# Attention probabilities turned in halves of 64 query rows, one half to each PSUM bank

## The reference

```python
s = jnp.einsum('bgrqd,bgkd->bgrqk', q, kc).astype(jnp.float32) * scale
p = jax.nn.softmax(s, axis=-1) if sink is None else softmax_with_sink(s, sink)
o = jnp.einsum('bgrqk,bgkd->bgrqd', p.astype(vc.dtype), vc)
```

## Time and profile before

| | before |
|---|---|
| median of three runs | 2024.0 us |
| profiled execution | 2020.81 us, its span 2018.9 us |
| TensorE matmul busy | 1805.2 us, 89% |
| TensorE weight load busy | 1390.1 us, 69% |
| VectorE busy | 1046.3 us, 52% |
| ScalarE busy | 606.0 us, 30% |
| GpSimd busy | 325.4 us, 16% |
| mean granted TensorE clock | 0.943 |

### The profile page before, as it was taken

The page is one execution under the profiler, slowest core; times in us unless marked ns, Lnnn a source line. Parts: engine busy times, 40 slices in busy tenths (PEclk is TensorE's granted clock), DMA queues, the critical chain, the costliest instruction groups (busy, mean ns, idle before and its releaser), DMA issues.

```text
span 2018.9 us, 26641 instructions
## 1 busy us (share of the span) xinstructions
PE 1805.2 (89%) x9754; PEld 1390.1 (69%) x9754; DVE 1046.3 (52%) x1994; ACT 606.0 (30%) x910; POOL 325.4 (16%) x416
## 2 busy tenths in 40 slices
PE   7869879899949999999899968997989689999994
PEld 1737546566838888888678856884667578887883
DVE  1535645574385676666544356266753534344442
ACT  1201035464332112211223333113543423233342
POOL 0231312232150000000000033014421400000002
PEclk9889989999969999999999988997999889999997
DMA  7665643112242443344221163334512333332233
GB/s 263 161 155 188 241 94 98 40 25 88 81 146 84 125 119 102 112 125 125 84 73 63 63 231 124 103 112 119 134 34 74 104 92 95 104 86 70 85 103 115
DMA packets 258124, 223.99 MB, mean 111 GB/s; under 512 B 67470, under 2 KB 218271, under 8 KB 258038
## 3 DMA queue, kind: packets, MB, share of 16 engines
q1 hardware_dynamic: 249156, 202.50, 33.2%
q0 software_dynamic: 7008, 18.79, 3.3%
q10 hardware_dynamic: 1876, 1.58, 0.3%
HBM read 193.58 MB, written 29.25 MB: 110 GB/s over the span
## 4 chain that ended last, share of the span: by engine, by line
PE 76%; DVE 11%; POOL 4%; issue 3%; DMA 3%; ACT 2%; SPq 0%; ACTq 0%; DVEq 0%; POOLq 0%
PE ps L995 31%; PE ps L676 9%; PE ps L677 9%; PE ps L678 9%; PE ps L848 4%; PE ps L890 4%; PE ps L927 3%; PE ps L690 2%; POOL arena L1832 2%; DVE arena L1604 2%; DVE arena L1568 1%; DVE arena L1396 1%; PE ps L719 1%; PE ps L700 1%; PE ps L882 1%
## 5 line engine op out<-in xcount | busy, mean ns | idle before, releaser
L1331 DVE TENSOR_TENSOR w_lo<-w_raw,w_hi 128x2048 fp32r<-128x2048 f32 (+3 forms) x114 | 209.6, 1839 | 353.0 <-ACT w_hi L1082 352.9
L676 PE MATMUL ps<-w_hi,act_hi 128*128 128x512 f32 (+2 forms) x952 | 371.9, 391 | 18.7 <-DVE act_lo L1331 17.8
L677 PE MATMUL ps<-w_lo,act_hi 128*128 128x512 f32 (+2 forms) x952 | 368.8, 387 | 0.0
L678 PE MATMUL ps<-w_hi,act_lo 128*128 128x512 f32 (+2 forms) x952 | 368.3, 387 | 0.0
L1082 ACT ACTIVATE w_hi<-w_raw 128x2048 fp32r<-128x2048 f32 (+3 forms) x114 | 176.6, 1550 | 552.0 <-PE ps L678 434.4
L995 PE MATMUL ps<-act_hi,w_hi 128*128 128x512 f32 (+1 forms) x1056 | 321.0, 358 | 2.8 <-DVE act_lo L1331 2.8
L995 PE MATMUL ps<-act_lo,w_hi 128*128 128x512 f32 (+1 forms) x1056 | 319.7, 357 | 0.0
L995 PE MATMUL ps<-act_hi,w_lo 128*128 128x512 f32 (+1 forms) x1056 | 319.2, 356 | 0.0
L676 PEld LDWEIGHTS ps<-w_hi,act_hi 128*128 128x128 f32 x952 | 182.7, 192 | 58.1 <-issue 15.8
L678 PEld LDWEIGHTS ps<-w_hi,act_lo 128*128 128x128 f32 x952 | 182.2, 191 | 34.7
L677 PEld LDWEIGHTS ps<-w_lo,act_hi 128*128 128x128 f32 x952 | 182.4, 192 | 34.0
(11 more groups left out here) (108 smaller groups left out, 1835.4 us busy)
## 6 DMA issues: line engine op xcount, KB each, us to landing
arena<-in_ada_w SPq DMA_DIRECT2D x44, 1024.0 KB, 8.7
w_raw<-in_ffn_up SPq DMA_DIRECT2D x88, 512.0 KB, 5.3
w_raw<-in_ffn_down SPq DMA_DIRECT2D x88, 256.0 KB, 2.7
w_raw<-in_odd_w_in SPq DMA_DIRECT2D x20, 512.0 KB, 4.6
arena<-mods SPq DMA_DIRECT2D x16, 512.0 KB, 6.7
proj_odd<-arena POOLq DMA_DIRECT2D x26, 256.0 KB, 2.5
x_after_mix<-arena SPq DMA_DIRECT2D x10, 512.0 KB, 2.9
arena<-x_after_mix SPq DMA_DIRECT2D x10, 512.0 KB, 4.2
```

Of the source, the lines that this page charges most:

```text
L676: mm(out_, s_hi, m_hi, start=start, stop=False)
L677: mm(out_, s_hi, m_lo, start=False, stop=False)
L678: return mm(out_, s_lo, m_hi, start=False, stop=stop)
L1331: V.tensor_sub(out_, full, hi.bitcast(fp32)).then_inc(sem_, 1)
```

## The change

The transposes of probabilities no longer split the key tiles over the two banks. Each tile is transposed in two parts: query rows 0 to 63 through array rows 0 to 63 into bank 6, and query rows 64 to 127 through array rows 64 to 127 into bank 7. Each part is a 64 by 128 stationary operand against a 64 by 64 identity. A bank then holds n pieces of 64 columns. Both banks are waited for ahead of the first part, and the two parts of the last tile signal the two banks. ScalarE and VectorE each copy n times 64 columns, into the 64-column halves of the tiles in SBUF. The preparation rounds are as they were.

```diff
@@ probs_t (TensorE)
                     v = (sunk if a.name == "swa" else biased)[k % 2][x][:, ROWS - n * P:ROWS]
-                    srcs = [v[:, c * P:(c + 1) * P] for c in range(n)]
-                    turns(a.unit_round[k, x], srcs[:(n + 1) // 2], srcs[(n + 1) // 2:])
+                    r = R0 + a.unit_round[k, x]
+                    at_least(pe, left_free, r)
+                    at_least(pe, right_free, r)
+                    for c in range(n):
+                        for g in range(2):
+                            half = slice(64 * g, 64 * g + 64)
+                            last = nc.tensor.transpose(bank(6 + g)[:, c * 64:(c + 1) * 64],
+                                                       v[half, c * P:(c + 1) * P], ident[half, half])
+                            if c == n - 1:
+                                last.then_inc((left_done, right_done)[g], 1)
@@ attention (ScalarE)
+                def left_rows(r, dst, n):
+                    act.wait_ge(left_done, R0 + r + 1)
+                    A(dst, bank(6, n * 64).rearrange("p (t r) -> p t r", r=64), ACT.Copy).then_inc(left_free, 1)
 ...
                 def probs(k, x):
-                    n = (len(keys_of(a.units[a.steps[k][1]])) + 1) // 2
+                    n = len(keys_of(a.units[a.steps[k][1]]))
                     at_least(act, pv_done, PV0 + V0 + k - 1)
-                    left(a.unit_round[k, x], pt[k % 2][x][:, 0:n, :].rearrange("p t r -> p (t r)"), n)
+                    left_rows(a.unit_round[k, x], pt[k % 2][x][:, 0:n, 0:64], n)
@@ attention (VectorE)
+                def right_rows(r, dst, n):
+                    dve.wait_ge(right_done, R0 + r + 1)
+                    V.tensor_copy(dst, bank(7, n * 64).rearrange("p (t r) -> p t r", r=64)).then_inc(right_free, 1)
 ...
-                    right(a.unit_round[k, x], pt[k % 2][x][:, (n + 1) // 2:n, :].rearrange("p t r -> p (t r)"), n // 2)
+                    right_rows(a.unit_round[k, x], pt[k % 2][x][:, 0:n, 64:128], n)
```

## The result

The change makes the kernel slower. Its median is 2041.03 us (2038.64 to 2042.62, four runs) against 2023.96 (2019.84 to 2025.72) for the kernel before beside it: ratio 1.0086, 95% interval 1.0067 to 1.0106. The forecast was 2035, in a range of its own of 2028 to 2042. The profiled execution took 2039.48, 18.7 more than the one of before; forecast were 10.9 more.

The account below looks back on a forecast made before the run. TensorE was the only engine near full, with waits between engines setting most steps. NA 5.1, SWA 8, MLA 0.4, GQA -0.6 and phase ends -2 made +10.9 on 2020.8: 2031.7, or 2035 on the median's scale, range 2028 to 2042.

Parts of the forecast that it names:

- The price of a record: Transposes of probabilities: a 64-row record takes 0.033 us, so six key tiles take 0.40 instead of 0.66.
- Rival A: Transposes in all four phases: halves don't pay in full, 0.053 us a record, 13 us more, 2048; chance 0.2.
- rival B: Transposes in all four phases: no overlap at all, 0.107 us a record, 75 us in all, 2099; chance 0.08.
- The wait: Head 1's turn moves behind VectorE's copy, delaying ScalarE's copy and exp: NA +5.1, SWA +8 us.
- the NA loop: NA's regular step: the loop through ScalarE takes 5.28 us against 4.96, +0.32, in ten of 16 steps.
- SWA's regular pair: SWA's six steps of a pair: together 2.0 us longer, four pairs +8.
- MLA's pair: MLA: small preparation steps lose 0.38 each, large steps gain 0.56 over two; three pairs at +0.2 us, phase +0.4.
- The drain: TensorE between array shapes: 0.09 to 0.15 us a change; in GQA four added changes a step, 0.45 together.
- GQA's sign: GQA steps: shorter turns outweigh the added shape changes, -0.07 us a step, -0.6 in all.
- The ends of the phases: Last two turns of each of four phases, with no minima in their way: each saves 0.26 us, -2 in all.
- Rival C: Attention phases: ScalarE's delay is absorbed and shorter turns pay on the path, faster at 2008; chance 0.08.
- D: Whole kernel: nothing measurable, 0.027 us a record and SWA's delay half hidden, +7, 2026; chance 0.14.

Follow-up runs that it names:

- the kernel with halves in turn: The changed kernel, but each head's row-0-to-63 records come first, waiting for bank 6 alone, then the others for bank 7: 2024.44 us, ratio 1.0014.
- the filler's run: The changed kernel plus a useless TensorE product ahead of head 1's turn in 40 of 48 MLA and SWA steps: 2051.17 us, ratio 1.0138.
- the whole-transposes run: The changed kernel in MLA, SWA and NA, with whole 128-row transposes in GQA: 2045.17 us, ratio 1.0101.
- e8: As e7, but head 0 alternates the row halves while head 1 keeps them in turn: 2025.97 us, ratio 1.0001.
- e7: The changed kernel with row halves one after the other, each waiting for its own bank, in MLA, SWA, NA; whole transposes in GQA: 2024.88 us, ratio 0.9997.

## Why the prediction was right, and where its sizes were off

**The price of a record** came out as taken. Twelve take 0.56 to 0.59 and one 0.223, (0.56 - 0.223)/11 = 0.031 to 0.033; 0.033 was taken. That it fits so closely is in part luck: the eight 32-row products of the earlier trace rows do not come at an even pace, they start as four at 343.84 and four at 344.05, and their 0.033 is the mean of one such gap. Rival A (0.053) and rival B (0.107) fall here. The rule that spoke for A, in the Trainium skill (TensorE: Matmul & The Clock Gate, LDWEIGHTS: a load's time is its columns over 1.2 GHz, by estimate 0.107 for 128 columns), is not what these loads show: six in a row in one half, in the kernel with halves in turn, are (0.45 - 0.139)/5 = 0.062 apart by their loads.

```profile
1457.28 0.45 PEld L910 LDWEIGHTS ps<-ident,arena 64*128 64x128 f32 x6 [0.17 <-issue]
```

**The wait** did what was said, and three runs show it from three sides: without the joint wait, with it alone, and with the exp out of its reach. By terms the NA loop was 2.28 + 0.55 + 0.06 + 0.80 + 0.39 + 1.04 + 0.16 = 5.28 forecast, and is 2.29 + 0.55 + 0.15 + 0.65 + 0.39 + 1.05 + 0.08 = 5.16. Turn to copy was put 0.15 too long: the 0.43 for a first record held the long form's own 0.27, where the short one's is 0.22, and it was read to VectorE's copy, which starts 0.05 behind ScalarE's. The start behind the copy was put 0.09 too short, the reciprocal 0.08 too long. NA steps with a preparation of Q grew by 0.28 and with one of K by 0.35 (forecast 0.25 and 0.37).

SWA's regular pair grew by 1.7 (forecast 2.0), and its steps one by one agree too: 0.46, 0.15, 0.27, 0.50, 0.48 and -0.17, against 0.37, 0.18, 0.37, 0.57, 0.51 and 0. (The step that the prediction calls two-key and bound by the outputs' copies turns four keys.) MLA's pair grew by 0.1 (forecast 0.2), which is the difference of larger parts: the two small steps with a preparation grew by 0.42 and 0.38 (forecast 0.38 each), the other four shrank by 0.70 together (forecast 0.56).

**The drain** was undersized, and that turned GQA's sign. A step's two turns last 0.52 each, of which 12 x 0.031 = 0.37 are records and 0.15 is not, and PV and the scores are 0.20 longer each: the four changes are 0.70, not 0.45, and the step is +0.12, not -0.07. The starts of single records tell where it lies. Ahead of a turn, PV's last product starts at 1543.13 and the first transpose at 1543.33, 0.21 apart instead of 0.11. Behind a turn, the last transpose starts at 1540.30, PV's first product at 1540.46 and its second at 1540.67; those two are 0.21 apart instead of 0.11. So entering costs 0.10, and leaving 0.15 and then 0.10 more behind the first product. The prediction took 0.09 to 0.15 a change from rows read only up to the first product behind it. The Trainium skill (TensorEngine Tiling (Array Packing), Key Properties) says that a change of mode drains the engine, and this trace agrees; here a turn pays 0.35 for its two changes.

**The ends of the phases** were to give 2 us and gave none that can be seen; at the end of GQA TensorE waits for VectorE's copy twice, 0.84 us each, where before it waited 0.41 for ScalarE's and 0.81 for VectorE's.

**The clock** is what the sum left out, and the prediction had named its fall as a cause outside it. Mean granted clock and the engines' busy time in the four phases, before and after (columns: stretch, its length, busy us and instructions of each engine, clock, DMA share, GB/s):

```profile
266.00:394.00 128.00, 119.55 (x1117) 78.21 (x1117) 70.63 (x206) 65.44 (x158) 36.62 (x48) 0.99 0.27 62
396.00:490.00 94.00, 85.71 (x724) 56.26 (x724) 63.17 (x219) 57.56 (x154) 31.49 (x48) 0.96 0.10 23
1386.00:1483.00 97.00, 87.14 (x738) 57.33 (x738) 61.89 (x202) 51.14 (x107) 43.24 (x39) 0.94 0.34 86
1486.00:1549.00 63.00, 56.76 (x366) 45.16 (x366) 28.81 (x70) 25.34 (x53) 14.49 (x16) 1.00 0.00 1
```

```profile
267.30:395.90 128.60, 106.58 (x1340) 72.26 (x1340) 69.48 (x205) 65.58 (x158) 36.62 (x48) 0.97 0.27 62
398.70:500.80 102.10, 74.36 (x900) 56.12 (x900) 62.64 (x217) 57.52 (x154) 31.49 (x48) 0.92 0.10 21
1395.80:1498.70 102.90, 73.89 (x930) 55.45 (x930) 60.72 (x202) 51.09 (x107) 43.09 (x39) 0.90 0.33 82
1502.10:1567.00 64.90, 57.23 (x462) 43.02 (x462) 27.97 (x69) 25.55 (x53) 14.48 (x16) 0.98 0.00 1
```

TensorE's busy share fell from 91% to 73% in SWA and from 90% to 72% in NA, and the clock with it: 48 us at 1.2 GHz in the four phases after, 23 before. What such a stretch does is seen in NA, where a preparation of K fell into one, and at the first scores of GQA:

```profile
1440.35 1.47 PE L848 MATMUL ps<-ident,arena 128*128 128x128 f32 x6 [0.61 <-ACT arena L1169]
...
1441.74 2.61 PE L890 MATMUL ps<-arena 64*128 64x512 f32 x8
...
1502.10 4.42 PE L882 MATMUL ps<-arena 128*128 128x384 f32 x8 [0.85 <-DVE arena L1580]
1507.58 2.85 PE L882 MATMUL ps<-arena 128*128 128x384 f32 x8 [1.06 <-DVE nb L1620]
```

The eight scores take 2.61 instead of 1.54, and the whole step 8.22 instead of 6.58; GQA's first scores 4.42 instead of 2.82. In NA and GQA the filler's run puts it at 2.3 and 1.6. In MLA it is one step of 6.92 for 5.66, 1.3. In SWA it is read less surely: one step of the last pair took 4.47 at a clock of 0.66, where the whole-transposes run, the same code there, took 3.09 (1.4), and in a later stretch PV took 2.40 for 1.31 and the turn behind it 0.69 for 0.47 (1.3): 2.7. Together 7.9 of the 19.1; what is left is MLA +0.1, SWA +6.2, NA +3.8, GQA +1.1, 11.2 against 10.9 forecast. The agreement of the sums hides two errors, and is luck so far: SWA and NA were put 2.1 too high, GQA 2.2 too low.

Not settled: what sets off the lower clock. Less busy time on TensorE goes with more of it in the changed kernel, but the joint wait alone, with NA 81% busy (86.3 of 106.0), had 17 us of it, and e8, whose NA step is as in e7, had 21 against 12. The changed kernel's own NA code had 21, 17 and 12 in three runs. No run holds the clock and leaves the rest, so the clock's 7.9 is read from steps and phases that met more of it, and why the change met more is not shown.

Rival C needed ScalarE's copy under 0.48 behind the free bank; it starts 0.80 behind (1476.10 to 1476.90). The 0.80 that the prediction had was counted from the turn's start, 0.06 later. D fell with the SWA delay, which came nearly in full.

## What to carry to other kernels

When two waits are joined ahead of one block, look at who reads the half that could have gone early, and what that engine runs next in order: here the joint wait cost 36 us (0.018 of 2022) and the faster transposes gave back half. An array shape that is used between others pays on entering and on leaving, 0.35 us a turn here, so shorten work in a shape only where the neighbours share it. Give a change that leaves TensorE idle more often a term of its own for the clock, and compare traces by the phases that the change can touch.

## What the runs showed of the hardware

- Transposes of 64 rows in alternating halves of the array go at 0.031 to 0.033 us each, six in a row in one half at 0.062 by their loads: two halves at once take no longer than one.
- A product of one row half starts while transposes of the other half are still running (1458.43 against 1458.84), and ahead of three of them that come earlier in the program.
- A turn of 64-row transposes between full 128-row products pays 0.35 us for its two changes of shape, measured where TensorE has no gap: 0.10 to enter, 0.15 to leave and 0.10 behind the first product after it.
- Two executions of the kernel before agreed within 0.04 us in each of four phases and differed by 8.1 us ahead of them.
